# Seven products for half of the feed-forward output, and a convolution split between ScalarE and VectorE

## The reference

```
def conv_glu_ffn(x, w_in, conv_w, conv_b, w_out):
    S = x.shape[1]
    h = x @ w_in
    hp = jnp.pad(h, ((0, 0), (CONV_WIDTH - 1, 0), (0, 0)))
    hc = conv_b + hp[:, 0:S] * conv_w[0]
    for kk in range(1, CONV_WIDTH):
        hc = hc + hp[:, kk:kk + S] * conv_w[kk]
    gate, val = jnp.split(hc, 2, axis=-1)
    return (jax.nn.gelu(gate, approximate=False) * val) @ w_out

x = layer_norm(DEEPNORM_ALPHA * x + ffn, ln_gain[layer, 1], ln_bias[layer, 1])
```

## Time and profile before

| | |
|---|---|
| median of three runs | 2062.64 us |
| the profiled execution, its span | 2061.1 us |
| around the span in a run (median less span) | 1.5 us |
| TensorE busy | 2052.3 us |
| VectorE busy | 1444.6 us |
| ScalarE busy | 887.1 us |
| one turn of the feed-forward loop | 66.22 us |
| weights moved, mean rate | 389.57 MB, 189 GB/s |

### The profile page before, as it was taken

The page is one execution under the profiler, slowest core; times in us unless marked ns, Lnnn a source line. Parts: engine busy times, 40 slices in busy tenths (PEclk is TensorE's granted clock), DMA queues, the critical chain, the costliest instruction groups (busy, mean ns, idle before and its releaser), DMA issues.

```text
span 2061.1 us, 27212 instructions
## 1 busy us (share of the span) xinstructions
PE 2052.3 (100%) x10924; PEld 1756.3 (85%) x10924; DVE 1444.6 (70%) x1641; ACT 887.1 (43%) x825; POOL 5.8 (0%) x10
## 2 busy tenths in 40 slices
PE   9999999999999999999999999999999999999998
PEld 8888888888888888888888877888888888888887
DVE  5446566767767687677697886786776768766768
ACT  5433443543443434434434555354344344444342
POOL 0000000000000000000000000000000000000000
PEclk9999999999999999999999999999999999999999
DMA  9654474655555565555555435465555555555552
GB/s 331 196 191 145 142 258 163 235 197 187 188 196 186 187 198 184 186 199 184 188 186 190 144 123 190 162 241 194 194 184 193 193 184 195 191 184 195 191 184 102
DMA packets 194766, 389.57 MB, mean 189 GB/s; under 512 B 6970, under 2 KB 9748, under 8 KB 193684
## 3 DMA queue, kind: packets, MB, share of 16 engines
q1 hardware_dynamic: 194419, 388.49, 56.6%
q10 hardware_dynamic: 288, 0.26, 0.1%
HBM read 386.36 MB, written 2.10 MB: 188 GB/s over the span
## 4 chain that ended last, share of the span: by engine, by line
PE 98%; DVE 1%; DMA 0%; SPq 0%; issue 0%; ACT 0%; DVEq 0%
PE ps L1270 36%; PE ps L1280 19%; PE ps L1297 13%; PE ps L1299 12%; PE ps L1298 12%; PE ps L1420 1%; PE ps L1711 1%; PE ps L1686 1%; PE ps L1694 1%; PE ps L1387 0%; PE ps L1425 0%; PE ps L1258 0%; PE ps L1537 0%; DMA xres<-x 0%; DVE xres L810 0%; PE ps L1338 0%
## 5 line engine op out<-in xcount | busy, mean ns | idle before, releaser
L475 ACT ACTIVATE w_hi<-raw 128x2048 fp32r<-128x2048 f32 x352 | 673.9, 1916 | 951.1 <-DMA raw<-ffn_w_in 523.7
L752 DVE TENSOR_TENSOR w_lo<-raw,w_hi 128x2048 fp32r<-128x2048 f32 x352 | 800.9, 2287 | 220.0 <-ACT w_hi L475 219.2
L1270 PE MATMUL ps<-T,w_hi 128*128 128x512 f32 x3264 | 765.0, 390 | 0.0
L1270 PEld LDWEIGHTS ps<-T,w_hi 128*128 128x128 f32 x3264 | 605.7, 188 | 122.9 <-issue 1.7
L1280 PEld LDWEIGHTS ps<-T,w_lo 128*128 128x128 f32 x3264 | 405.8, 192 | 10.0 <-issue 2.0
L1280 PE MATMUL ps<-T,w_lo 128*128 128x256 f32 x3264 | 410.6, 283 | 0.0
L1297 PE MATMUL ps<-w_hi,gT 128*128 128x512 f32 x704 | 274.2, 389 | 0.0
L1299 PE MATMUL ps<-w_hi,gT 128*128 128x512 f32 x704 | 273.9, 389 | 0.0
L1298 PE MATMUL ps<-w_lo,gT 128*128 128x512 f32 x704 | 273.9, 389 | 0.0
L782 DVE TENSOR_TENSOR arena<-ps,half 128x512 f32<-128x512 f32 x96 | 65.5, 688 | 183.6 <-ACT half L539 183.6
L786 DVE SCALAR_TENSOR_TENSOR xres<-ps,xres 128x1024 f32<-128x1024 f32 (+1 forms) x103 | 117.9, 1144 | 89.1 <-PE ps L1299 87.9
(11 more groups left out here) (159 smaller groups left out, 802.9 us busy)
## 6 DMA issues: line engine op xcount, KB each, us to landing
raw<-ffn_w_in SPq DMA_DIRECT2D x176, 1024.0 KB, 5.0
raw<-ffn_w_out SPq DMA_DIRECT2D x88, 1024.0 KB, 5.0
raw<-even_w_in SPq DMA_DIRECT2D x38, 1024.0 KB, 5.1
raw<-attn_w_qkv SPq DMA_DIRECT2D x20, 1024.0 KB, 5.2
raw<-even_w_out SPq DMA_DIRECT2D x16, 1024.0 KB, 5.0
raw<-attn_w_out SPq DMA_DIRECT2D x16, 1024.0 KB, 5.1
arena<-ln_gain SPq DMA_DIRECT2D x4, 1024.0 KB, 6.3
arena<-ln_bias SPq DMA_DIRECT2D x4, 1024.0 KB, 8.3
```

The lines of the kernel that those rows point to most:

```text
L475: nc.scalar.activation(w_hi[:, s % RING], raw[:, s % RING], ACT.Copy).then_inc(hi_ready, 1)
L752: vec.tensor_tensor(w_lo[:, s % RING], raw[:, s % RING], w_hi[:, s % RING].bitcast(F32), ALU.subtract).then_inc(lo_ready, 1)
L1270: ins = mm(ps[:, banks[j]], w_hi[:, s % RING, k, P * j:P * j + P], T[:, GK * kg + k], start=kg == 0 and k == 0, stop=kg == KG - 1 and k == ...
```

## The change

**Output.** The chunks 0 to 9 of a layer are taken in five pairs, called duos. For a duo the output in column blocks 0 and 1 is a product of 2 x 2 blocks: two token halves by two chunks (activations X_11, X_21, X_12, X_22, first index the token half) times two chunks by two column blocks (weights W_11, W_12, W_21, W_22). It is computed with seven products of sums (Strassen's scheme in Winograd's form) in place of eight. Column blocks 2 and 3 stay as they were, with both chunks of the duo accumulated in PSUM before they are added. The eleventh chunk is computed as before.

**Slots.** The order in a layer is now: gate and value of chunks 0 and 1; then for each duo gate and value of the next chunk, seven slots for the products, gate and value of the chunk after that, four slots for column blocks 2 and 3. A product slot has 12 matmuls. Four of the seven slots use a sum of weights, which DVE computes in float32 before ACT rounds it: SUM_12 = W_11 + W_12, SUM_24 = W_12 + W_22 (in place in the ring), SUM_124 and SUM_ALL. Three of these have no load of their own; they lie in the space of the gain and bias, which are loaded later now. The loads of the ring are numbered apart from the slots (`LOAD_OF`).

**Activations.** The four sums and differences D_1 to D_4 of activations are made by DVE; each of the eight forms is rounded by ACT and gets its remainder from DVE. PE's products wait until all eight are there.

**Results.** DVE adds the products to `xres` in nine readings (`take_product`) of 512 elements. Two banks are read and then accumulated further: product 3 (W_22) goes on in the bank of product 1, product 5 (SUM_124) in that of product 2, product 7 in that of product 4. Each waits for the reading of what was there.

**Convolution.** ACT multiplies by the three taps (`scale_taps`: six instructions on 256 elements for two blocks of 128 columns), DVE adds (`add_taps`: two instructions on 512 elements).

**Form.** The loops over turns are written out.

```diff
-FFN_GROUPS = 3 * KG * FC
+DUOS = FC // 2
+PRODUCTS = 7
...
+for chunk in (0, 1):
+    place(G_AT, chunk, KG)
+    place(V_AT, chunk, KG)
+for duo in range(DUOS):
+    place(G_AT, 2 * duo + 2, KG)
+    place(V_AT, 2 * duo + 2, KG)
+    place(Q_AT, duo, PRODUCTS)
+    if 2 * duo + 3 < FC:
+        place(G_AT, 2 * duo + 3, KG)
+        place(V_AT, 2 * duo + 3, KG)
+    place(C_AT, duo, KG)
+TAIL_AT = FFN_GROUPS
+FFN_GROUPS += NCH
...
+SUM_12, W_11, W_22, SUM_24, SUM_124, W_21, SUM_ALL = range(PRODUCTS)
+SUM_PLACES = {SUM_12: 1, SUM_124: 0, SUM_ALL: 1}
+SUM_COUNTS = {SUM_12: 1, SUM_24: 2, SUM_124: 3, SUM_ALL: 4}
+SUMS = {S_FFN[l] + Q_AT[p] + i: (i, 4 * (DUOS * l + p) + n)
+        for l in range(2) for p in range(DUOS) for i, n in SUM_COUNTS.items()}
+SLOT_OF = [s for s in range(S_END) if s not in SUMS or SUMS[s][0] == SUM_24]
+LOAD_OF = {s: i for i, s in enumerate(SLOT_OF)}
+FORMS = 8
+X_11, X_21, D_3, X_12, X_22, D_1, D_2, D_4 = range(FORMS)
+FORM_AT = {X_12: 0, X_22: 1, D_1: 2, D_2: 3, D_3: 4, D_4: 5}
+READS = 9
...
+        def raw_at(s):
+            if s in LOAD_OF:
+                return raw[:, LOAD_OF[s] % RING]
+            return lnp[:, SUM_PLACES[SUMS[s][0]]].rearrange("p (k n) -> p k n", k=GK)
+        def lo_at(s):
+            return w_lo[:, LOAD_OF[s] % RING] if s in LOAD_OF else sum_lo[:, SUM_PLACES[SUMS[s][0]]]
+        def landed(s):
+            return raw_landed[LOAD_OF[s] % RING], 16 * (LOAD_OF[s] // RING + 1)
...
-            def load(s, source, turn=0):
-                if not isinstance(turn, int) or s >= RING:
-                    sp.wait_ge(used, s - RING + 1 + turn * 12)
-                sp.dma_start(raw[:, s % RING], source).then_inc(raw_landed[s % RING], 16)
+            def load(s, source):
+                i = LOAD_OF[s]
+                if i >= RING:
+                    sp.wait_ge(used, SLOT_OF[i - RING] + 1)
+                sp.dma_start(raw[:, i % RING], source).then_inc(raw_landed[i % RING], 16)
...
+                for p in range(DUOS):
+                    a, b = 2 * p, 2 * p + 1
+                    chunk(a + 2)
+                    q, s = base + Q_AT[p], base + C_AT[p]
+                    out_block(l, q + W_11, a, 0)
+                    out_block(l, q + W_22, b, 1)
+                    out_block(l, q + SUM_24, a, 1)
+                    out_block(l, q + W_21, b, 0)
+                    if b + 2 < FC:
+                        chunk(b + 2)
+                    for i in range(KG):
+                        out_block(l, s + i, (a, b)[i % 2], 2 + i // 2)
...
+                def scale_taps(c, value, q):
+                    n = tp + 4 * c + 2 * value + q
+                    act.wait_ge(added, n + 1)
+                    if value and c >= 2:
+                        act.wait_ge(form_ready, FORMS * (DUOS * l + (c - 2) // 2 + 1))
+                    elif c >= 1:
+                        act.wait_ge(gated_out, gp + 2 * (c - 1) + q + 1)
+                    to = gated[:, c % 2] if value else conv_g
+                    for i in range(2):
+                        t = 2 * q + i
+                        at = (FT // 2) * value + TPC * c + t
+                        tap = lambda row: taps[:, 4 * l + row, at:at + 1]
+                        nc.scalar.activation(to[:, t], h[:, t, 0:SEQ], ACT.Identity, bias=tap(3), scale=tap(0))
+                        nc.scalar.activation(half[:, n % 2, i], h[:, t, 1:1 + SEQ], ACT.Copy, scale=tap(1))
+                        ins = nc.scalar.activation(scaled_2[:, n % 2, i], h[:, t, 2:2 + SEQ], ACT.Copy, scale=tap(2))
+                    ins.then_inc(scaled, 1)
...
+                    s = base + V_AT[a]
+                    kind_halves(a, 0, x, s)
+                    for q in range(2):
+                        scale_taps(a, 0, q)
+                    for j in range(KG):
+                        high(s + j + HI_LEAD)
                         if j in (1, 2):
-                            gated_high(gp + j, j - 1, turn)
-                        if j in (5, 6):
-                            gelu(gp + 2 + j - 4, j - 5, turn)
...
-            def convolve(kind, q, conv, cur, bank, n, turn=0):
-                t = 2 * q
-                if bank is not None:
-                    pair_sum(h[:, t:t + 2, CONV - 1:], n, bank, turn)
-                dve.wait_ge(added, n + 1 + turn * 4)
-                for k in range(CONV):
-                    for i in (t, t + 1):
-                        if k == 0:
-                            ins = vec.tensor_scalar(conv[:, i], h[:, i, 0:SEQ], cur[:, kind, 0, i:i + 1],
-                                                    cur[:, kind, 3, i:i + 1], ALU.mult, ALU.add)
-                        else:
-                            ins = vec.scalar_tensor_tensor(conv[:, i], h[:, i, k:k + SEQ],
-                                                           cur[:, kind, k, i:i + 1], conv[:, i],
-                                                           ALU.mult, ALU.add)
-                    if k < CONV - 1 or kind == 1:
-                        chain(ins)
-                    else:
-                        ins.then_inc(conv_done, 1)
...
+                def add_taps(c, value, q, conv):
+                    n, i = tp + 4 * c + 2 * value + q, 4 * (FC * l + c) + 2 * value + q
+                    to = conv[:, 2 * q:2 * q + 2]
+                    dve.wait_ge(scaled, i + 1)
+                    chain(vec.tensor_tensor(to, to, half[:, n % 2], ALU.add))
+                    vec.tensor_tensor(to, to, scaled_2[:, n % 2], ALU.add).then_inc(conv_done, 1)
...
+                def weight_sums(p):
+                    q, n = base + Q_AT[p], 4 * (DUOS * l + p)
+                    dve.wait_ge(*landed(q + W_11))
+                    dve.wait_ge(*landed(q + SUM_24))
+                    vec.tensor_tensor(raw_at(q + SUM_12), raw_at(q + W_11), raw_at(q + SUM_24), ALU.add) \
+                        .then_inc(summed, 1)
+                    dve.wait_ge(*landed(q + W_22))
+                    vec.tensor_tensor(raw_at(q + SUM_24), raw_at(q + SUM_24), raw_at(q + W_22), ALU.add) \
+                        .then_inc(summed, 1)
+                    dve.wait_ge(summed, n + 1)
+                    vec.tensor_tensor(raw_at(q + SUM_124), raw_at(q + SUM_12), raw_at(q + W_22), ALU.add) \
+                        .then_inc(summed, 1)
+                def last_weight_sum(p):
+                    q, n = base + Q_AT[p], 4 * (DUOS * l + p)
+                    dve.wait_ge(*landed(q + W_21))
+                    dve.wait_ge(summed, n + 3)
+                    vec.tensor_tensor(raw_at(q + SUM_ALL), raw_at(q + SUM_124), raw_at(q + W_21), ALU.add) \
+                        .then_inc(summed, 1)
+                def take_product(p, i, bank, a, n, sign, before=0):
+                    r, c = READS * (DUOS * l + p), slice(COLS * n, COLS * n + COLS)
+                    if before:
+                        dve.wait_ge(quad_read, r + before)
+                    vec.scalar_tensor_tensor(xres[:, a, c], ps[:, bank], sign / ALPHA, xres[:, a, c],
+                                             ALU.mult, ALU.add).then_inc(quad_read, 1)
...
+                    s = base + V_AT[a]
+                    kind_sums(a, 0, x)
+                    for j in range(KG):
+                        if j == 1:
+                            weight_sums(p)
+                        low(s + j + LO_LEAD)
+                        if j < 2:
+                            gate_pair(a, j)
+                    s = base + Q_AT[p]
+                    low(s + LO_LEAD)
+                    dve.wait_ge(used, s + 1)
+                    last_weight_sum(p)
+                    take_product(p, 0, x, 1, 1, -1.0)
+                    low(s + 1 + LO_LEAD)
+                    dve.wait_ge(used, s + 2)
+                    take_product(p, 1, x + 1, 0, 0, 1.0)
+                    low(s + 2 + LO_LEAD)
+                    dve.wait_ge(used, s + 3)
+                    take_product(p, 2, x, 0, 1, -1.0)
+                    low(s + 3 + LO_LEAD)
+                    dve.wait_ge(used, s + 4)
+                    take_product(p, 3, x + 3, 1, 1, -1.0, 1)
+                    low(s + 4 + LO_LEAD)
+                    dve.wait_ge(used, s + 5)
+                    take_product(p, 4, x + 1, 0, 1, -1.0, 3)
+                    take_product(p, 5, x + 1, 1, 0, 1.0)
+                    take_product(p, 6, x + 1, 1, 1, -1.0, 4)
+                    dve.wait_ge(used, s + 6)
+                    take_product(p, 7, x + 2, 0, 0, 1.0, 2)
+                    dve.wait_ge(used, s + 7)
+                    take_product(p, 8, x + 3, 1, 0, 1.0, 6)
+                    low(s + 5 + LO_LEAD)
+                    low(s + 6 + LO_LEAD)
...
+            def form_product(s, f, bank, start, stop=True, more=False):
+                for k in range(GK):
+                    x_hi, x_lo = form_at(f)[:, k, 0], form_at(f)[:, k, 1]
+                    w, last = w_hi[:, s % RING, k], stop and k == GK - 1
```

(56 more changed lines are left out.)

507 lines of the change are left out of this document (316 added, 191 removed).

## The result

The changed kernel takes 2084.55 us (median of four runs, 2082.78 to 2095.37) against 2062.61 us before: ratio 1.0117, 95% interval 1.0098 to 1.0137. It is slower, by 22 us where 3.8 were forecast, and outside the forecast range. The result has three terms: ten gaps, a clock that falls behind some of them, and a slower pace of part of the new matmuls. The profiled execution took 2083.62 us, its span is 2081.8.

What follows compares the result with a forecast made beforehand. PE was taken as the bound (busy 2052.3 of 2061.1 us): 27.2 us gained against 10 gaps of 3.1, 31 us, gives +3.8, from 2062.64 to 2066.4 us. Forecast 2062.4 to 2070.4 had 0.70; the range ran from 2059 to 2074.

Steps and rivals of the forecast that it cites:

- What bounds the kernel, and the matmuls removed: Whole kernel: PE bounds it, so removing 120 matmuls at 0.2267 us each gains 27.2 us.
- The place and length of the gap: Seven products: PE waits 3.1 us before product 3 for DVE's first reading, ten times, 31 us.
- landing, chain and ScalarE's scalings: Before product 3: weights land at -11.37, DVE's instructions in order end at 8.23; ACT's scalings cost 2.7 us per pair.
- The clock falls in the ten gaps: Rival: 1.2 GHz for 12 matmuls behind each gap, 27 us more, 2093; for five products, 2200. Chance 0.03.
- the prediction's own signs of being wrong: PE waiting for a product's rounding or remainder, at another product or in a hidden block, or lower clock behind gaps.
- unrolled code: Rival: PE's products in unrolled code run at a pace other than 0.23 us per matmul. Chance 0.01.
- the clearly slower rival: DVE hand-overs from load landing to first reading cost extra: 0.1 us each gives 2077, 0.2 gives 2088. Chance 0.14.
- VectorE's load: DVE over the whole kernel: totals near 95 of some 130 us a duo, busy time near 1450.
- The transition to the last chunk and the later gain and bias: Last chunk's block: at most 0.5 us more a layer, counted as nothing; later gain and bias loading has over 2 us cover.

Runs made afterwards that it cites:

- undoing runs: Changed kernel with second tap additions ahead of the weight sums (2062.81 us), first reading ahead of the last weight sum (2059.09 us), or both (2046.36 us).

## Why the prediction was wrong

The profiled execution was forecast at 2066.4 us and took 2083.6, 17.2 more. The gaps were 1.6 us shorter than forecast (29.4 against 31), the clock cost 7.8 us and the pace 9.4; 1.6 us are not accounted for. Either of the two missing terms alone would have carried the time beyond 2070.4.

- **What bounds the kernel, and the matmuls removed: right.** 120 fewer; with the gap closed 16 of the 27.2 us arrive, and the pace takes 9.4 of the rest.
- **The place and length of the gap: right.** Product 3, ten times, 2.94 us in the mean where 3.1 was worked out; landing, chain and ScalarE's scalings (2.6 us a pair, 2.7 assumed) as computed. The undoing runs moved it by the amounts of the chain.
- **The first step that failed: the clock, put at nothing in the sum.** "The clock falls in the ten gaps" stood as a rival with a chance of 0.03, on the ground that PE is busy on both sides. The trace had no gap longer than 0.9 us once the kernel had started, so it gave no ground for so small a chance. The mechanism is real in five gaps of ten in the profiled execution, 7.8 us, and by the granted clock low for longer in two of the other three runs. A lower clock behind the gaps was one of the prediction's own signs of being wrong. Its price was also mis-sized: not twelve matmuls at double length but eight (1.55 us, not 2.7). The rule of the Trainium skill that was weighed there (TensorE: Matmul & The Clock Gate, Part 1, "What's actually happening"), that the throttled clock is the default and activity releases it, fits the run with idle products, where work in the gap held the clock up in nine duos of ten.
- **The second, and the larger: the pace of the new matmuls.** All were priced at 0.2267 us; those with a standing operand in forms take 0.232 to 0.234, and with the twelves from gT behind them that is 9.4 us. I gave a slower pace of the new products a chance of 0.01, as "unrolled code", and did not ask where the operands lie.
- **Hand-overs on VectorE: the clearly slower rival was wrong.** They cost nothing beyond the pitch, 19.6 us as summed, and would have explained the time by a wrong cause: 2084 by gaps alone wants 4.9 us, the trace has 2.9.
- **VectorE's load was mis-added.** Its busy time is 1521 us, not near 1450: the additions save 1.2 us a pair, 9.6 a duo, where the total of 95 us a duo can only have come from taking off twice that (94 before, 20 added). It cost nothing in the changed kernel, since VectorE idles elsewhere.
- The transition to the last chunk and the later gain and bias: no wait, as forecast.

## What to carry to other kernels

A slot of PE that becomes half as long needs the helpers' work for it halved as well, or moved to where they idle: here one group of additions and one reading, put elsewhere in VectorE's order, turn 22 us of loss into 16 of gain (2046.4), and other places in memory make it 19 (2043.8). Price a hole in a dense matmul stream with what the clock may add behind it, unless the trace shows a hole of that length without a fall. And look at the pace of new matmuls by operand before using the old one.

## What the runs showed of the hardware

- TensorE's clock behind holes in an otherwise dense stream: with gaps of 0.5 to 0.8 and of 1.5 to 1.8 us no fall in ten each; of 2.7 to 3.1 us five in ten in one kernel and seven in ten in another, in the first with the longest spared and the shortest not; of 4.0 to 5.3 us twenty in twenty, in two kernels. A fall costs 1.55 us, some eight matmuls at 0.43 us in place of 0.23; four of the twenty cost 2.2 to 2.5. In the profiled changed kernel the low level starts up to 1.4 us behind the end of the gap; behind gaps of 4 us and more it can start inside them, by up to 2 us. With matmuls of 128 columns in the first 2 us of the gap there was one fall in ten, in the longest gap (4.0 us).
- A matmul of 512 columns takes 0.2267 to 0.2342 us depending on where its operands lie in the on-chip memory (byte addresses in a partition, `w_hi` for the moving operand; a third of the matmuls stream a remainder from elsewhere). Slow: standing operand at 187360, 195552 or 211936 with the moving one at 99456 and, for 195552, at 50304. Fast: standing at 148608 with moving at 99456; at 52416 and at 208064 with moving at 158912. Both fast pairs hold in the slots for column blocks 2 and 3; in and behind the products that stream from `sum_lo` the same standing operands take 0.230 to 0.232. What sets the pace is open; the address modulo 64 moves it by 0.0013 us in forms, not by the whole 0.0075. No more places were tried.
